# Final norm, transposes and stores issued between the units of the last MLP product

## The reference

```
h = rms_norm(x, norm2_gain) * (1 + sc2) + sh2
ff = square(relu(h @ w_ff1)) @ w_ff2
x = x + g2 * ff
y = rms_norm(x, final_gain)          # over the 1024 channels of each token
```

## Time and profile before

| | us |
|---|---|
| Median of 3 runs | 1898.38 |
| Lowest and highest run | 1896.92, 1898.89 |
| Span of the profiled execution | 1896.5 |
| TensorE busy in it | 1737.3 (92%) |
| VectorE busy | 1036.7 (55%) |
| ScalarE busy | 543.5 (29%) |
| GpSimd busy | 389.2 (21%) |
| Granted TensorE clock, mean | 0.940 of full speed |

### The profile page before, as it was taken

The page is one execution under the profiler, slowest core; times in us unless marked ns, Lnnn a source line. Parts: engine busy times, 40 slices in busy tenths (PEclk is TensorE's granted clock), DMA queues, the critical chain, the costliest instruction groups (busy, mean ns, idle before and its releaser), DMA issues. The chain is left out here.

```text
span 1896.5 us, 31647 instructions
## 1 busy us (share of the span) xinstructions
PE 1737.3 (92%) x13112; PEld 1499.8 (79%) x13112; DVE 1036.7 (55%) x1381; ACT 543.5 (29%) x780; POOL 389.2 (21%) x292
## 2 busy tenths in 40 slices
PE   7589889968987998599979999999999999999996
PEld 7568778867876887487868888888888888888885
DVE  7870574666357626844675455544445554444555
ACT  2231322812371256225344111112211111221103
POOL 4556544653464437000000000000000000000000
PEclk7589999989998998799989999999999999999997
DMA  6614223332333232611011111011111101111003
GB/s 238 237 62 189 102 100 125 127 134 77 134 132 107 77 142 106 239 63 56 1 56 45 45 45 37 8 44 44 44 44 44 39 5 44 44 44 44 34 1 122
DMA packets 43940, 155.62 MB, mean 82 GB/s; under 512 B 6976, under 2 KB 11584, under 8 KB 43584
## 3 DMA queue, kind: packets, MB, share of 16 engines
q1 hardware_dynamic: 38800, 132.91, 19.9%
q10 hardware_dynamic: 5040, 21.22, 2.8%
HBM read 118.19 MB, written 35.92 MB: 81 GB/s over the span
## 5 line engine op out<-in xcount | busy, mean ns | idle before, releaser
L1556 DVE SCALAR_TENSOR_TENSOR x<-bank,mod,x 128x512 f32<-128x512 f32 (+1 forms) x384 | 246.1, 660 | 145.7 <-PE bank L97 144.4
L95 PE MATMUL bank<-h_hi,in_lo 128*128 128x512 f32 (+1 forms) x768 | 293.0, 381 | 14.7 <-issue 6.5
L96 PE MATMUL bank<-h_lo,in_hi 128*128 128x512 f32 (+1 forms) x768 | 281.4, 366 | 0.0
L97 PE MATMUL bank<-h_hi,in_hi 128*128 128x512 f32 (+1 forms) x768 | 280.8, 366 | 0.2 <-issue 0.2
L95 PE MATMUL bank<-h_hi,up_lo 128*128 128x512 f32 (+1 forms) x768 | 272.9, 355 | 8.7 <-DVE h_lo L410 6.3
L96 PE MATMUL bank<-h_lo,up_hi 128*128 128x512 f32 (+1 forms) x768 | 272.8, 355 | 0.0
L97 PE MATMUL bank<-h_hi,up_hi 128*128 128x512 f32 (+1 forms) x768 | 272.2, 354 | 0.0
L96 PE MATMUL bank<-hid_lo,down_hi 128*128 128x256 f32 x720 | 256.1, 356 | 0.0
L95 PE MATMUL bank<-hid_hi,down_lo 128*128 128x256 f32 x720 | 255.5, 355 | 0.0
L97 PE MATMUL bank<-hid_hi,down_hi 128*128 128x256 f32 x720 | 254.6, 354 | 0.0
L95 PEld LDWEIGHTS bank<-h_hi,in_lo 128*128 128x128 f32 x768 | 153.6, 200 | 39.1 <-issue 9.1
(11 more groups left out here) (208 smaller groups left out, 2592.4 us busy)
## 6 DMA issues: line engine op xcount, KB each, us to landing
proj<-mx_stage ACTq DMA_DIRECT2D x32, 640.0 KB, 3.0
up_raw<-in_w_ff SPq DMA_DIRECT2D x34, 512.0 KB, 5.7
in_raw<-in_w_in SPq DMA_DIRECT2D x32, 512.0 KB, 4.7
mx_ada_raw<-in_w_ada SPq DMA_DIRECT2D x32, 512.0 KB, 3.5
down_raw<-in_w_ff SPq DMA_DIRECT2D x30, 512.0 KB, 3.3
ada_raw<-in_w_ada SPq DMA_DIRECT2D x16, 512.0 KB, 4.4
x_scratch<-x_first SPq DMA_DIRECT2D x1, 5120.0 KB, 15.8
mx_q<-proj SPq DMA_DIRECT2D x8, 640.0 KB, 6.3
```

Of the source, the lines that this page charges most:

```text
L95: nc.tensor.matmul(out, w_lo, x_hi, start=start, stop=False)
L96: nc.tensor.matmul(out, w_hi, x_lo, start=False, stop=False)
L97: return nc.tensor.matmul(out, w_hi, x_hi, start=False, stop=stop)
L1556: nc.vector.scalar_tensor_tensor(xs, g.bank[3 + u % DOWN_BANKS][:, 0:n], g.m(40 + m, int(b > 0)), xs, ALU.mult, ALU.add).then_inc(unit_add ...
```

## The change

The output stage is gone as a stage; its work is issued inside the MLP's block, around the last down product.

- The last down product takes its units in another order: `last_unit(u)` gives `u % 8` as the tile m and `LAST_BLOCKS[u // 8]` as the block, with `LAST_BLOCKS = (1, 2, 0)`. So all eight tiles of block 1 come first, then block 2, then block 0. VectorE's additions follow the same order.
- `turn_after(i)` gives the unit behind which TensorE turns the i-th chunk (in the order block 1, block 2, block 0): 9, 11, 13, 15 for the four chunks of block 1, 17, 19, 21, 23 for those of block 2, and 23 for the two of block 0.
- A turn first waits until all units of its block have been added (`block_added`). There are two pairs of banks for the chunks (0 with 1, and 2 with 7), so turn i also waits for the scaling of chunk i - 2.
- ScalarE's order is as before: squares of chunk i + 1, then root of chunk i.
- VectorE issues the half sums of chunk i behind the addition of unit `turn_after(i) + 1`, and behind that of unit `turn_after(i) + 2` the reciprocal and at once the scaling of the same chunk i. What has no such unit comes behind the last one, chunk by chunk.
- The scaled chunks have a tile of their own for each (`y`, 40 KB per partition, where `h_hi` lay), so no scaling waits for a store. The gain row lies where `h_lo` lay and is loaded by SP behind the last weights, once the last up product has read `h_lo`.
- SP stores each chunk when it is scaled, in the order of the turns.

```diff
+        LAST_BLOCKS = (1, 2, 0)
+        y = at(nc, "y_tok", [P, CHUNKS, D_MODEL], F32, 0)
...
+        y_order = [c for b in LAST_BLOCKS for c in chunks_of(b)]
+        y_banks = lambda i: (g.bank[(0, 2)[i % 2]], g.bank[(1, 7)[i % 2]])
+
+        def last_unit(u):
+
+            return u % KT, LAST_BLOCKS[u // KT]
+
+        def turn_after(i):
+
+            done = sum(len(chunks_of(b)) for b in LAST_BLOCKS[:1])
+            return (KT if i < done else 2 * KT) + 2 * (i % done) + 1 if i < 2 * done else UNITS - 1
+
+        def block_added(eng, i):
+
+            block = [y_order[i] in chunks_of(b) for b in LAST_BLOCKS].index(True)
+            for r in range(DOWN_BANKS):
+                eng.wait_ge(unit_added[r], (pairs - 1) * PER + (block + 1) * KT // DOWN_BANKS)
...
         @block.sync
...
+            sp.wait_ge(up_used[1], pairs)
+            sp.dma_start(gain[:, :], a["final_gain"].broadcast_to([P, D_MODEL])).then_inc(gain_in, 16)
+            for i, c in enumerate(y_order):
+                t = c * P
+                sp.wait_ge(scaled, 2 * i + 2)
+                sp.dma_start(a["y_prompt"][t:t + P, :] if t < CTX else a["y_sample"][t - CTX:t - CTX + P, :],
+                             y[:, c, :]).then_inc(stored, 16)
+            sp.wait_ge(stored, 16 * CHUNKS)
...
         @block.scalar
...
+            def square(i):
+                act.wait_ge(turned, i + 1)
+                for half in range(2):
+                    if i:
+                        act.wait_ge(y_squared, 2 * i + half - 1)
+                    nc.scalar.activation(squares[:, half, :], y_banks(i)[half][:, :], ACT.Square,
+                                         accum_out=sums[:, i, half:half + 1]).then_inc(y_squared, 1)
+            square(0)
+            for i in range(CHUNKS):
+                if i + 1 < CHUNKS:
+                    square(i + 1)
+                act.wait_ge(totalled, i + 1)
+                nc.scalar.activation(root[:, i:i + 1], total[:, i:i + 1], ACT.Sqrt, bias=g.eps[:, 0:1],
+                                     scale=1.0 / D_MODEL).then_inc(rooted, 1)
...
         @block.vector
...
-            add(pairs - 1, range(UNITS))
+
+            def add_sums(i):
+                dve.wait_ge(y_squared, 2 * i + 2)
+                nc.vector.tensor_tensor(total[:, i:i + 1], sums[:, i, 0:1], sums[:, i, 1:2], ALU.add
+                                        ).then_inc(totalled, 1)
+
+            def scale(i):
+                dve.wait_ge(rooted, i + 1)
+                nc.vector.reciprocal(rstd[:, i:i + 1], root[:, i:i + 1]).then_inc(rstd_ready, 1)
+                dve.wait_ge(rstd_ready, i + 1)
+                for half in range(2):
+                    part = slice(half * D_MODEL // 2, (half + 1) * D_MODEL // 2)
+                    nc.vector.scalar_tensor_tensor(y[:, y_order[i], part], y_banks(i)[half][:, :], rstd[:, i:i + 1],
+                                                   gain[:, part], ALU.mult, ALU.mult).then_inc(scaled, 1)
+            for u in range(UNITS):
+                add(pairs - 1, (u,), last_unit)
+                for i in range(CHUNKS):
+                    if turn_after(i) + 1 == u:
+                        add_sums(i)
+                    if turn_after(i) + 2 == u:
+                        if i == 0:
+                            dve.wait_ge(gain_in, 16)
+                        scale(i)
+            for i in range(CHUNKS):
+                if turn_after(i) + 1 >= UNITS:
+                    add_sums(i)
+                if turn_after(i) + 2 >= UNITS:
+                    scale(i)
...
         @block.tensor
...
+            def turn(i):
+                block_added(pe, i)
+                if i >= 2:
+                    pe.wait_ge(scaled, 2 * (i - 2) + 2)
+                c = y_order[i]
+                for f in range(KT):
+                    last = nc.tensor.transpose(y_banks(i)[f // 4][:, (f % 4) * P:(f % 4 + 1) * P],
+                                               g.x[:, f, c * P:(c + 1) * P], g.ident[:, :])
+                last.then_inc(turned, 1)
...
-            down_product(pairs - 1, 1, up)
+            down_product(pairs - 1, 1, up, last_unit, turns_after)
...
-        output(nc, g, a)
```

More of the change, by code:

```diff
@@ L1448, in mlp @@
         pairs = FF_BLOCKS // 2
+        LAST_BLOCKS = (1, 2, 0)
+        y = at(nc, "y_tok", [P, CHUNKS, D_MODEL], F32, 0)
+        gain, squares = at(nc, "y_gain", [P, D_MODEL], F32, 40), at(nc, "y_squares", [P, 2, D_MODEL // 2], F32, 44)
+        sums, total = at(nc, "y_sums", [P, CHUNKS, 2], F32, 48), at(nc, "y_total", [P, CHUNKS], F32, 48.5)
+        root, rstd = at(nc, "y_root", [P, CHUNKS], F32, 49), at(nc, "y_rstd", [P, CHUNKS], F32, 49.5)
+        gain_in, turned, y_squared, totalled, rooted, rstd_ready, scaled, stored = (
+            sem(n) for n in ("gain_in", "turned", "y_squared", "totalled", "rooted", "rstd_ready", "scaled", "stored"))
+        chunks_of = lambda b: range(TOK_BLOCKS[b][0] // P, sum(TOK_BLOCKS[b]) // P)
+        y_order = [c for b in LAST_BLOCKS for c in chunks_of(b)]
[9 more added lines that the diff above has]
+                eng.wait_ge(unit_added[r], (pairs - 1) * PER + (block + 1) * KT // DOWN_BANKS)
         block = ctx.enter_context(nc.Block())
@@ L1546, in _, with add @@
             step(pairs - 2, 0)
+            def square(i):
[12 more added lines that the diff above has]
+                                     scale=1.0 / D_MODEL).then_inc(rooted, 1)
         @block.vector
         def _(dve):
-            def add(p, units):
+            def add(p, units, place=lambda u: divmod(u, 3)):
                 for u in units:
-                    m, b = divmod(u, 3)
+                    m, b = place(u)
                     t0, n = TOK_BLOCKS[b]
@@ L1594, in up_product, with down_product @@
                         last.then_inc(up_used[s] if b == 2 else full[b], 1)
-            def down_product(p, parity, weights=down):
+            def down_product(p, parity, weights=down, place=lambda u: divmod(u, 3), after=lambda u: None):
                 if weights is down:
@@ L1612, in down_product, with turns_after @@
                     last.then_inc(unit_full[u % DOWN_BANKS], 1)
+                    after(u)
+            def turn(i):
[7 more added lines that the diff above has]
+                last.then_inc(turned, 1)
+            def turns_after(u):
+                for i in range(CHUNKS):
+                    if turn_after(i) == u:
+                        turn(i)
             norm.tensor(pe)
```

## The result

The changed kernel is slower: 1903.85 us in the median of 5 runs (1901.98 to 1904.61) against 1896.92 for the kernel before beside it, a ratio of 1.0032 with a 95% interval of 1.0020 to 1.0043. The ratio is taken over all runs of both kernels and is not the quotient of the two medians: they lie 6.9 us apart, the ratio says 6.1 us (3.8 to 8.2). A second series later gave 1.0042 (1.0028 to 1.0056). The profiled execution's span is 1902.0 us, its run took 1903.85.

A forecast was written before the change was run, and what follows sets the result against it. A chain through TensorE, ScalarE and VectorE sets the pace: 51.28 + 4.19 + 2.15 + 3.07 = 60.69 us after 1838.16 gives 1898.85; 1.82 for the clock and 1.9 around the span make 1902.6 us, range 1899.5 to 1906.5.

The forecast's parts named there:

- The order of the units at 0: Last down product: taking its 24 units in block order 1, 2, 0 costs 0, still 27.7 us of matmuls.
- The gain load and the block boundary: Ahead of the old output stage: the gain load's 5.41 us disappear under matmuls and the boundary's 1.42 us go.
- The closed chain: Turns in the last product: turn, squares, root, reciprocal, scaling, next turn set the pace, 4.24 us a round at full clock.
- The last matmul: End of the last down product: last matmul around 1881 instead of 1865.6, the last unit done at t = 42.7.
- The clock: Last turns: turns 8 and 9 run at the half clock after longer idle times, 1.8 us; ends 0 and 5.5.
- rival B: Turns among short units: the clock falls there, 1906.2 us in all, as little as 1903.5 if later; chance 0.25.
- The tail: From turn 9's start to the span's end: 4.19, 2.15 for chunk 9 alone and 3.07 us behind the last scaling.
- Rival A: Turns in the last product: TensorE's own pace, rounds of 3.66 and 2.36 us, holds; 1892.1 us in all; chance 0.07.

The follow-up runs named there:

- order_only: The kernel before with only the last product's units in the new order and the old output stage; ratio to before 1.0003.
- root_first: The changed kernel with ScalarE taking the root of chunk i before the squares of chunk i+1; 1884.58 us, ratios to before 0.9926 and 0.9939.
- four_slots: The changed kernel with 4 of 8 transposes a turn, into one bank, so a turn waits for the scaling of chunk i-4; 1885.80 us, ratio to before 0.9936.
- filled: The changed kernel with useless matmuls in TensorE's idle times ahead of turns 4 to 9; 1901.25 us, ratio to before 1.0016.
- one_wait: The changed kernel with the `block_added` waits only at turns 0, 4 and 8; 62.62 us from the last product's first matmul to the end.

## Why the prediction was right

It said 1902.6 us, slower by 4.2 through a chain that closes over three engines; measured were 1903.85, with 5.1 us more in the end stage and 6.1 by the ratio. The mechanism is the one that was forecast. That the two totals lie only 1.25 us apart is in part luck: the forecast stands on a median of 1898.38 for the kernel before, and beside the changed kernel that median was 1896.92. By its steps:

*The order of the units at 0*: shown by order_only. *The gain load and the block boundary*: the load was issued at 1811.06 and nobody waited for it.

*The closed chain*: shown from both legs (root_first, four_slots) and by filled, where added work on TensorE cost nothing. Link by link at the full clock: turn to squares 1.10 us (predicted 1.10), squares to reciprocal 1.48 (1.48), reciprocal to scaling 0.20 (0.20), scaling to the next turn 1.56 against 1.41 + 0.05. The last link was mis-sized by 0.1, as its row came from a turn with a single wait; eight rounds make 0.8 us of it. one_wait shows that the four waits of `block_added` are that 0.1 in the link.

*The last matmul* was put at 1881, with the last unit done at t = 42.7. That is a slip: units 22 and 23 stand behind turn 6 and ahead of turn 7, so by the forecast's own rounds they end at 38.56 + 0.92 + 1.44 = 40.9. The last matmul started at 41.18 (1879.73). The sum does not use this number. (The 30.7 us from the last matmul to the end, also unused, are 30.9 from its start and 30.5 from its end.)

*The clock*: I took two turns at 1.2 GHz. It fell within turn 7, so about two and a half: 2.2 us against 1.8. Four idle times of 1.85 us came ahead of turns 4 to 7, and the clock fell in turn 7 and not only behind it; in one_wait it outlasted turn 7. The 2.2 us lie between the forecast and the least that rival B allowed (1903.5, which is three turns or 2.7 us); B's own condition, a fall among the short units, did not come true in any of the three profiles. The forecast also read its row too coarsely: behind the idle time of 3.16 us the turn began at the full clock (1874.27; the earlier trace rows have 1.00 until 1874.90), and its two turns took 3.41 us, not the 3.98 of later ones. So in the kernel before, too, the clock fell within a turn, 0.6 us behind its start.

By the Trainium skill (TensorE: Matmul & The Clock Gate, Part 4: PE-mode transpose) transposes do not count as busy time for the clock in the way that matmuls do. These traces do not bear that out. Among the short units TensorE had 1.44 us of matmuls in each 4.34, and the clock stayed at full from the end of turn 3 (1865.57) to the start of turn 7 (1881.85), some 16 us. And in order_only the clock rose from 1.2 to 2.4 GHz at 1885.1, some 16 us after the last matmul that was not a transpose.

*The tail*: forecast were 9.41 us from the last turn's start at the full clock; filled has 9.28 (1888.72 to 1898.0).

*Rival A*, TensorE's own pace, did not come true in the changed kernel. It was priced at 52.0 us of end stage; root_first brings that pace about, with 46.6. Of the 5.4 us less, 3.8 are the last two rounds, which I had left at the length of the full chain and which the other order also opens (2.43 and 2.25 us instead of 4.24), and 1.9 the tail behind the last turn (7.55 instead of 9.41); turn 7 came 0.25 later than priced. The reason given against A, the order that is written out, was the right one.

*Sum.* The end stage grew by 5.11 us where 4.17 were forecast. Of the 0.94 between them, 0.80 are the last link and 0.38 the clock, less 0.24 in the tail and up to turn 1. What the medians show beyond that stays open.

## What to carry to other kernels

Where a pipeline is given fewer buffers, check on paper whether one engine's order "next item first, then finish this one" now meets the wait for a free buffer. Here, with four slots (four_slots), that order held nothing up; with two, chunk i could not be finished before the turn of chunk i + 1, and turn i + 2 not start before chunk i was finished. The sign in this profile is a constant distance between items whatever work lies between, with idle times on every engine of the chain. And measure such a change by the stretch it touches: here the medians scattered by more than the effect of some edits, while the stretch repeated to 0.03 us, or 0.16 where the clock fell within it.

## What the runs showed of the hardware

- Waits that are already fulfilled are not free behind a wait that holds TensorE: four of them ahead of the one that held it added 0.1 us (0.15 against 0.05 from the scaling's end to the turn).
- Eight 128 x 128 float32 transposes took 1.06 us at 2.4 GHz (from the first's start to the last's end) and 1.94 at 1.2 GHz; 32 in one piece took 3.68 at 2.4 GHz.
- The granted clock rose from 1.2 to 2.4 GHz in a stretch in which TensorE did nothing but such transposes (order_only, 1885.1).
- Matmuls of no use in the idle times kept the clock at 2.4 GHz and were worth 2.2 us in 63; opening the chain was worth more than seven times that.
- Issuing the last store in two halves of 256 KB gained nothing (45.42 against 45.48 us): the DMA engines, 0.96 busy at 375 GB/s, were still moving the store before them when the first half was issued.
